# Projections of x and of the mixer's output in fp32r parts, on one Trainium2 core

## What is computed

```python
h = rms_norm(x, norm_mix_g)
proj = h @ w_in                     # 1024 x 2304: q, k, v (512 each), x_rg, gate_rg, q_ca (256 each)
o_sb = stick_breaking_attention(...)   # 8 heads of 64, strictly causal
o_rg = gelu(gate_rg) * rg_lru(conv(x_rg))
o_ca = memory_cross_attention(q_ca, mem, ...)  # 4 heads, softmax over 256 memory tokens
y = concat([rms_norm(o_sb, g_out_sb), rms_norm(o_rg, g_out_rg), rms_norm(o_ca, g_out_ca)])
x = x + y @ w_out                   # 1024 x 1024
x = x + moe_ffn(rms_norm(x, norm_ffn_g), ...)  # 64 experts (3 MB each), top 8 a token, one shared
```

## Time and profile before

| | us |
|---|---|
| runs | 619.40, 619.62, 621.31; median 619.62 |
| profiled execution | 622.31, its span on the core 620.5 |
| TensorE busy | 568.3 (92%), weight loads 368.6 |
| VectorE, ScalarE, GpSimd busy | 202.0, 139.7, 20.3 |
| transfers | 228.1 MB, mean 368 GB/s |
| chain that ended last | TensorE 57%, transfers 24%, SP's queue 12% |

### The profile page before, as it was taken

The page is one execution under the profiler, slowest core; times in us unless marked ns, Lnnn a source line. Parts: engine busy times, 40 slices in busy tenths (PEclk is TensorE's granted clock), DMA queues, the critical chain, the costliest instruction groups (busy, mean ns, idle before and its releaser), DMA issues.

```text
span 620.5 us, 9982 instructions
## 1 busy us (share of the span) xinstructions
PE 568.3 (92%) x4044; PEld 368.6 (59%) x4045; DVE 202.0 (33%) x516; ACT 139.7 (23%) x263; POOL 20.3 (3%) x78
## 2 busy tenths in 40 slices
PE   7999998999999998995999999899988999599775
PEld 5888774457566556662676565656655665356351
DVE  2247686777225222221222212112222122022102
ACT  4454246343111111110111101111111111011101
POOL 1003131000000000000000000000000000000000
PEclk8999999999999999997899999999999999899987
DMA  8995359633899999999999999999999999999992
GB/s 341 424 393 205 136 222 360 285 120 145 345 397 388 383 423 421 420 421 422 421 421 419 420 421 417 421 423 420 421 420 421 420 421 421 421 420 419 421 372 94
DMA packets 34143, 228.13 MB, mean 368 GB/s; under 512 B 3888, under 2 KB 4016, under 8 KB 8624
## 3 DMA queue, kind: packets, MB, share of 16 engines
q1 hardware_dynamic: 33952, 227.46, 89.5%
q10 hardware_dynamic: 144, 0.02, 0.0%
HBM read 226.42 MB, written 1.05 MB: 367 GB/s over the span
## 4 chain that ended last, share of the span: by engine, by line
PE 57%; DMA 24%; SPq 12%; ACT 2%; DVE 2%; issue 2%; ACTq 0%
DMA cell_gu<-in_w_up_e 16%; PE ps L1584 16%; SPq L355 9%; PE ps L1606 9%; PE ps L1336 7%; PE ps L1558 5%; DMA cell_gu<-in_w_gate_e 5%; PE ps L1614 5%; PE ps L1458 4%; PE ps L1353 4%; DMA cell_d<-in_w_down_e 2%; PE ps L1505 2%; PE ps L1343 1%; SPq L452 1%; DMA wA<-in_w_qk 1%
## 5 line engine op out<-in xcount | busy, mean ns | idle before, releaser
L1584 PE MATMUL ps<-cell_gu,xg 128*64 128x256 f32 (+2 forms) x2048 | 196.6, 404 | 30.2 <-DMA cell_gu<-in_w_up_e 20.0
L1584 PEld LDWEIGHTS ps<-cell_gu,xg 128*64 128x64 f32 (+2 forms) x2048 | 127.5, 133 | 106.0 <-issue 59.0
L1606 PE MATMUL ps<-cell_d,e_hT 128*64 128x512 f32 (+2 forms) x512 | 96.6, 611 | 5.0 <-issue 3.6
L1221 DVE TENSOR_TENSOR e_h<-e_sg,ps 128x256 f32<-128x256 f32 x26 | 16.1, 619 | 197.2 <-ACT e_sg L754 197.2
L1282 DVE SCALAR_TENSOR_TENSOR ylo<-ps,gslot,yhi 128x512 fp32r<-128x512 f32 x52 | 39.0, 751 | 121.7 <-ACT yhi L768 121.7
L1606 PEld LDWEIGHTS ps<-cell_d,e_hT 128*64 128x64 f32 (+2 forms) x512 | 28.2, 127 | 59.1 <-issue 56.4
L768 ACT ACTIVATE yhi<-ps,gslot 128x512 fp32r<-128x512 f32 x52 | 35.7, 687 | 121.8 <-PE ps L1606 121.8
L754 ACT ACTIVATE e_sg<-ps 128x256 f32<-128x256 f32 x26 | 10.0, 384 | 219.8 <-PE ps L1584 219.8
L1558 PE MATMUL ps<-pick,xhi 128*128 128x256 f32 x208 | 45.3, 299 | 1.1 <-DVE pick L1139 1.1
L1614 PE MATMUL ps<-yhi,S 128*128 128x512 f32 x104 | 43.3, 417 | 0.6 <-DVE ylo L1282 0.6
L1558 PE MATMUL ps<-pick,xlo 128*128 128x256 f32 x208 | 41.9, 283 | 0.0
(11 more groups left out here) (315 smaller groups left out, 496.6 us busy)
## 6 DMA issues: line engine op xcount, KB each, us to landing
cell_gu<-in_w_gate_e SPq DMA_DIRECT2D x64, 1024.0 KB, 26.2
cell_gu<-in_w_up_e SPq DMA_DIRECT2D x64, 1024.0 KB, 26.6
cell_d<-in_w_down_e SPq DMA_DIRECT2D x60, 1024.0 KB, 27.2
wA<-in_w_qk SPq DMA_DIRECT2D x8, 512.0 KB, 10.6
wo<-in_w_out SPq DMA_DIRECT2D x1, 4096.0 KB, 13.3
cell_d<-in_w_down_e SPq DMA_DIRECT2D x8, 512.0 KB, 17.3
wR<-in_w_rest SPq DMA_DIRECT2D x3, 1024.0 KB, 28.0
wV<-in_w_v SPq DMA_DIRECT2D x1, 2048.0 KB, 17.6
```

What stands on the lines that cost most here:

```text
L1221: nc.vector.tensor_tensor(dst[:].rearrange("q k p -> q p k"), e_sg[:].rearrange("q (p k) -> q p k", k=KH), ps[:, U, DE:2 * DE].rearrange(" ...
L1584: last = mm(ps[side * w:(side + 1) * w, U, cols], rows(k, slice(side * w, (side + 1) * w)), cell_gu[i][:, k, :], start=k == 0, stop=k == K ...
L1606: last = mm(ps[side * w:(side + 1) * w, Y[half], :], e_hT[:, kk, side * w:(side + 1) * w], cell_d[n][:, kk, half * 512:(half + 1) * 512], ...
```

## The change

Twelve blocks of x (2 to 7, 10, 11, 14 to 17) no longer run as fp32 products. Their weights are split: ScalarE casts the high part (`split_q`, `split_r`), GpSimd subtracts it and leaves the low part in the weight's own place. The two parts of `hT` lie side by side in one tile `h_both`, so that one fp32r product of 512 columns makes high by high and high by low at once, in the two halves of the bank, and one of 256 columns adds low by high to the first half. VectorE sums the two halves (`reduce_sum`) before it scales. Block 10's bank is now emptied by VectorE instead of ScalarE.

The output projection runs in three fp32r terms. ScalarE's scaling of y writes the high part, VectorE makes the low part (`low_y`), `split_o` casts the weights' high part into cells 8 to 11 of the ring, four casts of 1024 elements a partition in the walk behind `gelu` and one behind each softmax head, and GpSimd subtracts. In GpSimd's program the adds of squares of the first group move ahead of the last four subtractions, and the building of the order tables behind them.

Loads move: expert 1's gate and up go to other cells, and wait for block 1 and the squares of x; down of experts 1 and 2, and expert 3's gate and up, go behind block 17; expert 4's gate and up, and down of experts 3 and 4, behind the output projection.

```diff
-    cell_of = dict(zip(loads, [0, 1, 16, 4, 17, 5, 3, 2, 6, 9, 7, 10, 8, 11, 12, 13, 14, 15]))
+    cell_of = dict(zip(loads, [0, 1, 6, 4, 7, 5, 3, 2, 16, 9, 17, 10, 8, 11, 12, 13, 14, 15]))
...
+    h_both = at("h_both", o_ring + 16 * KB, [P, 2, KD, SEQ], F32R)
+    hT_hi, hT_lo = h_both[:, 0], h_both[:, 1]
...
+    wo_hi = [at(f"wo_hi{k}", o_ring + (72 * KB + 4 * KB * k if k < 6 else 40 * KB + 4 * KB * k), [P, D], F32R) for k in range(KD)]
...
-        walk = [("unit", 0), ("unit", 1), ("row", 0), ("unit", 2), ("unit", 3), ("unit", 4), ("split_w", 0), ("unit", 5),
-                ("split_w", 1), ("unit", 6), ("mem_norm", 0), ("unit", 7), ("split_a", 1)]
+        walk = [("unit", 0), ("unit", 1), ("split_q", 2), ("row", 0), ("split_q", 3), ("unit", 2), ("split_q", 4), ("unit", 3),
+                ("split_q", 5), ("split_q", 6), ("unit", 4), ("split_w", 0), ("split_q", 7), ("unit", 5), ("split_w", 1), ("unit", 6),
+                ("mem_norm", 0), ("unit", 7), ("split_r", 2), ("split_a", 1)]
...
-            walk += {2: [("split_w", 2)], 3: [("split_w", 3)], 5: [("log1p", 0)], 7: [("ca_square", 0)], 8: [("ca_norm", 0)], 9: [("conv", 0)],
-                     11: [("gelu", 0)]}.get(i, [])
+            walk += {2: [("split_w", 2)], 3: [("split_w", 3)], 5: [("split_r", 0), ("log1p", 0)], 6: [("split_r", 1)], 7: [("ca_square", 0)], 8: [("ca_norm", 0)], 9: [("conv", 0)],
+                     11: [("gelu", 0), ("split_o", 0), ("split_o", 1)], 12: [("split_o", 2), ("split_o", 3)]}.get(i, [])
...
+            sp.wait_ge(unit_ps, 2)
+            sp.wait_ge(alo_dve, 1)
             load_fixed("gate", 1)
+            sp.wait_ge(ssq_act, 2)
             load_fixed("up", 1)
...
             sp.wait_ge(wo_ps, len(projections))
+            load_fixed("gate", 4)
+            load_fixed("up", 4)
+            load_fixed("down", 3)
+            load_fixed("down", 4)
             load_fixed("gate", 5)
...
+            def split_q(n):
+                pool.wait_ge(part_hi_act, n - 1)
+                pool.tensor_tensor(wA_lo[n][:], wA[n][:], wA_hi[n % 4][:].bitcast(F32), ALU.subtract).then_inc(part_lo_pool, 1)
+
+            def split_r(g):
+                pool.wait_ge(part_hi_act, (8, 9, 7)[g])
+                for c in (slice(0, 4), slice(4, 8)):
+                    hi, lo = (w2_both[:, 0, c, :], w2_both[:, 1, c, :]) if g == 2 else (wR_hi[g][:, c, :], wR_lo[g][:, c, :])
+                    pool.tensor_tensor(lo, wR[g][:, c, :], hi.bitcast(F32), ALU.subtract).then_inc(part_lo_pool, 1)
+
+            def split_o(k):
+                pool.wait_ge(part_hi_act, 10 + k)
+                pool.tensor_tensor(wo_lo[:, k, :], wo[:, k, :], wo_hi[k][:].bitcast(F32), ALU.subtract).then_inc(part_lo_pool, 1)
...
+            pool.wait_ge(ysq_act, 4)
+            link(pool.tensor_tensor(y_sq[:, 0:2, :], y_sq[:, 0:2, :], y_sq[:, 2:4, :], ALU.add))
+            pool.tensor_tensor(y_sq[:, 0, :], y_sq[:, 0, :], y_sq[:, 1, :], ALU.add).then_inc(ysum_pool, 1)
+            for k in range(4, KD):
+                split_o(k)
...
+                    if n in IN_PARTS:
+                        src = dst
+                        link(nc.vector.reduce_sum(src, b.rearrange("p (i s) -> p s i", i=2), AX.X))
+                    nc.vector.tensor_tensor(dst, src, rstd_row[:], ALU.mult).then_inc(unit_dve, 1)
...
+                    for k in range(KD):
+                        mm(b, hi[:, k, c:c + P], h_both[:, :, k, :], start=k == 0, stop=k == KD - 1, skip_group_check=True)
+                        last = mm(b[:, 0:SEQ], lo[:, k, c:c + P], hT_hi[:, k, :], start=False, stop=k == KD - 1,
+                                  skip_group_check=True)
...
-                        pe.wait_ge(yg_act, k + 1)
-                    last = mm(ps[:, ACC[2 * t + half], :], yT[:, k, t * P:(t + 1) * P],
-                              wo[:, k, half * 512:(half + 1) * 512], start=k == chunks[0], stop=k == chunks[-1])
+                        pe.wait_ge(alo_dve, 1 + KD + k + 1)
+                        pe.wait_ge(part_lo_pool, 12 + k + 1)
+                    q, c = slice(t * P, (t + 1) * P), slice(half * 512, (half + 1) * 512)
+                    for m, (y, w) in enumerate(((yT_hi[k][:, q], wo_hi[k][:, c]), (yT_lo[:, k, q], wo_hi[k][:, c]),
+                                                (yT_hi[k][:, q], wo_lo[:, k, c]))):
+                        last = mm(ps[:, ACC[2 * t + half], :], y, w, start=k == chunks[0] and m == 0,
+                                  stop=k == chunks[-1] and m == 2)
```

More of the change, by code:

```diff
@@ L178, in hybrid_decoder_layer @@
     yT = r("yT", [P, KD, SEQ])
+    yT_lo = at("yT_lo", r.offset - KD * SEQ * 4, [P, KD, SEQ], F32R)
+    yT_hi = [at(f"yT_hi{k}", (o_V + 12 * KB if k < 4 else o_R + 12 * KB) + KB * (k % 4), [P, SEQ], F32R) for k in range(KD)]
     x1 = at("x1", o_O, [P, NT, D])
@@ L413, in _ @@
             sp.dma_start(x1[:], x[0].rearrange("(t p) d -> p t d", p=P)).then_inc(x1_loaded, 16)
+            sp.wait_ge(unit_ps, 18)
+            load_fixed("down", 1)
+            load_fixed("down", 2)
+            load_fixed("gate", 3)
+            load_fixed("up", 3)
             sp.wait_ge(o_ps, SB_HEADS)
@@ L418, in _ @@
             load_shared("up")
[L419 to L424, removed]
             sp.wait_ge(unit_ps, 26)
@@ L507, in _, with edges @@
             pool.memset(grp[:], HUGE).then_inc(consts, 1)
[L509 to L516, removed]
-            for kind, h in walk:
+            def edges():
+                pool.wait_ge(xT_act, KD // 2)
+                pool.wait_ge(xT_dve, KD // 2)
+                pool.wait_ge(alo_dve, 1 + KD)
+                for b in range(2):
+                    link(pool.memset(rest[b][:, P:P + 1], 1.0))
+                    last = pool.memset(rest[b][:, NZ + 1:NZ + 2], 1.0)
+                    link(last)
+                pool.memset(stat[:, 15:16], 0.0).then_inc(zeroed, 1)
+            def split_q(n):
[9 more added lines that the diff above has]
+                pool.tensor_tensor(wo_lo[:, k, :], wo[:, k, :], wo_hi[k][:].bitcast(F32), ALU.subtract).then_inc(part_lo_pool, 1)
+            for kind, h in walk:
+                if kind == "split_o":
+                    split_o(h)
+                if kind == "split_q":
+                    split_q(h)
+                elif kind == "split_r":
+                    split_r(h)
                 if kind != "z":
                     continue
+                if h == 0:
+                    edges()
                 pool.wait_ge(bc_act, 2 * h + 2)
@@ L637, in split_w, with split_q, split_r @@
                 nc.scalar.copy((wV_hi, w_kv_hi)[i // 2][:, c, :], (wV, w_kv)[i // 2][:, c, :]).then_inc(whi_act, 1)
+            def split_q(n):
+                act.wait_ge(wA_loaded[n], 16)
+                if n >= 6:
+                    act.wait_ge(unit_ps, n - 3)
+                nc.scalar.copy(wA_hi[n % 4][:], wA[n][:]).then_inc(part_hi_act, 1)
+            def split_r(g):
+                act.wait_ge(wR_loaded[g], 16)
+                act.wait_ge(unit_ps, 8 if g == 2 else 12)
+                nc.scalar.copy(w2_both[:, 0] if g == 2 else wR_hi[g][:], wR[g][:]).then_inc(part_hi_act, 1)
             split_a(0)
@@ L1339, in unit @@
                     if n in (10, 11):
-                        pe.wait_ge(wR_loaded[2], 16)
+                        pe.wait_ge(part_lo_pool, 8)
                         c = (n - 10) * P
                         for k in range(KD):
-                            last = mm(b[:, 0:CA], hT[:, k, c:c + P], wR[2][:, k, :], start=k == 0, stop=k == KD - 1)
+                            mm(b, hT_hi[:, k, c:c + P], w2_both[:, :, k, :], start=k == 0, stop=k == KD - 1, skip_group_check=True)
+                            last = mm(b[:, 0:CA], hT_lo[:, k, c:c + P], w2_both[:, 0, k, :], start=False, stop=k == KD - 1,
+                                      skip_group_check=True)
                     else:
```

91 lines of the change are left out of this document (58 added, 33 removed).

## The result

The changed kernel takes 654.5 us (median; the kernel before on the same chips 620.4): ratio 1.055, interval 1.053 to 1.058. The forecast was 627.6 with a range of 619.5 to 634.0. The sign was right, the size was not: 34 us were lost where 8 were expected.

A forecast was written before the change was run, and what follows sets the result against it. The mixer's end, when group 0's gate product frees cells for the weights' stream, sets the time. Block 33 +9 and pairs -1.3 gave 7.8, taken as 8.0: 619.6 + 8.0 = 627.6 us, range 619.5 to 634.0.

The forecast's parts named there:

- the fixed rest: After group 0's gate product frees its cells: remaining weights' stream and tail, so each mixer microsecond is one of the result.
- ScalarE's start on y: Before the output projection: two VectorE sums, 1.4 us, delay y's block 2, so ScalarE begins at 90.6, +0.8 us.
- TensorE's saving: Blocks of x save 8.1 us and the output projection 6.4, together 14.5 us, if nothing else is late.
- rival (c): Whole mixer: low parts always ready, TensorE stays the bound; 14.5 us less, 605.1; chance 0.13, whole or in part.
- (a): Mixer: GpSimd and VectorE don't disturb each other; block 33 at about 119.8, total 621.1, 1.5 us slower; chance 0.18.
- To the first scores: 0: Start to first scores, 42.97 before: block savings offset by waits for low parts; 0 taken, best -0.9, upper case +6.
- deciding point: Whether VectorE's product after block 2's sum starts on time: 0.4 us or up to 2.8, deciding between forecast and (b).
- GpSimd's pace: A GpSimd subtraction of 1024 elements takes 2.37 us, from 2.14 ns an element and 0.18 fixed.
- its chain: GpSimd from 93.9: subtractions, adds, subtractions, order tables, second group's add; 26.2 us to 120.1, ahead of block 33.
- TensorE's waits for low parts: TensorE idle ahead of output projection and block 33, GpSimd named as releaser; no such waits would prove the prediction wrong.
- The term of contention, 6 us: Last GpSimd chain: GpSimd stands still while VectorE reads two SBUF tiles; 6 us taken between 0 and 10.4.
- rival (b): GpSimd's subtractions also stop VectorE, 2.4 us at a time; first scores 6 us later, total 633.6; chance 0.20.

The follow-up runs named there:

- Fills: Changed kernel with GpSimd's 20 subtractions replaced by about equally long fills of zero that read nothing from SBUF, low parts left out: 633.3 us, ratio 1.020.

## Why the prediction was right or wrong

**What bounds the kernel, and the fixed rest: right.** The end of the mixer moved by 34.3, the time by 34; the window behind it is 23.7 us in both, and the moved loads are hidden. Wrong is where the 8 us of the mixer were to come from. The forecast had ScalarE's start on y 0.8 us later, measured are 12.4 (102.2 for 89.77); it had the end of GpSimd's add for the second group about 10 us later, measured are 33.5 (149.2 for 115.69).

**TensorE's saving: right in size for a pair, wrong in where it would count.** A pair of products takes 0.352 us after (starts at 28.16, 28.51, 28.86) for 0.348 forecast. The output projection's saving was put too high: its four groups of three products take 2.84 us in the kernel without subtractions (100.90 in its chain), for 2.7 forecast and 3.44 before, so it is 0.15 a group rather than 0.2. How far the saving can get shows in the kernel without subtractions. ScalarE starts on y at 83.85 there, for 89.77 before, so 5.9 us had been won. Then come these (ScalarE's timeline, and the chain of waits):

```profile
86.33 3.87 ACT L707 CAST wo_hi<-wo 128x1024 fp32r<-128x1024 f32 x4
```

```profile
93.84 2.23 DVE yT_lo L1096 x3
```

The four casts stand ahead of the gates' sigmoids. These start at 91.51, for 93.31 before: of the 5.9 us, 4.1 are gone. The low parts of y stand ahead of the projections, and these ahead of the softmax scores in TensorE's queue: the first row maximum is at 98.15, for 97.87 before, and the rest is gone too. The first exponential (99.08, before 99.30) and the second group's add of squares (115.13, before 114.97) are level. So rival (c), 605.1, was out of reach for any speed of GpSimd in this order of work: free low parts of the weights give 622.3. I had both in the sum, but as something behind which GpSimd was later still. That the two alone eat the gain I hadn't drawn; the nearest case, (a), gave 621.1 for another reason.

**"To the first scores: 0": the first step that failed.** They start at 48.37 instead of 42.97. The text had this very case as its upper bound, +6, by "two or three times 2.4 us" in front of the memory parts, and measured are +5.4, with `wV_lo` (+2.2) and `memT_lo` (+3.8) in the chain. I took the lower end since the trace of before showed VectorE slowed by 0.09 us at most. (The deciding point that I had named, VectorE's product after block 2's sum, takes 1.93 us, at 21.22 in its timeline, for 0.42.) The row that gave the 0.09 had GpSimd instructions of 0.29 us beside it. It spoke of what short instructions do. An instruction that is stopped is stopped until the other one ends, and the change made that length eight times larger.

**GpSimd's pace: right, 5% too low; its chain: wrong.** 2.37 us were forecast for 1024 elements, by a line through two sizes; measured are 2.489, the mean of six, and 2.499, of eight. That the chain behind y would set the end was wrong: in the changed kernel the second group's add of squares comes at

```profile
148.49 0.73 POOL L601 TENSOR_TENSOR y_sq<-y_sq 128x256 f32<-128x256 f32 x1 [0.72 <-ACT y_sq L701]
```

released by ScalarE's square, not by the tables or subtractions ahead of it, which had ended 0.72 us before. GpSimd also had idle time in the chain that I drew without a gap: its four last subtractions wait 7.5 and 4.8 us for casts, which stand behind exponentials that wait for VectorE's `mx`. And TensorE's waits for low parts, whose absence was to be a sign of being wrong, come to 3.6 us.

**The term of contention, 6 us: the step of the sum that failed by most.** It was worked out as what GpSimd loses to VectorE's instructions, bounded by 10.4. What VectorE loses to GpSimd's was left out of it, although it is the larger side: 31 us more busy time, and 32.5 us of time (622.3 to 654.8) where TensorE waits for none of the subtractions. And rival (b) had it in kind, with the right sign and the right deciding point (a product beside a subtraction takes 2.5 us instead of 0.43: row `beta` above), but counted it only up to the first scores, +6. It works in every stage of the mixer in which a subtraction runs: the convolution +5.9 (three of its six `xc` take 2.4 to 2.5 us, for 0.484), the little chain of `lam` +6 (L903, L911 and L912 at 2.0, 2.3 and 2.3 for 0.16 to 0.17), the row maxima and `ca_p`. 20 subtractions of 2.5 us are 50 us in which such an instruction can't run, and the question to ask was how many of VectorE's instructions would come up in them. The windows of before had much of the answer. VectorE was busy for 29.0 of the 40 us from 60 to 100 and for 12.8 of 16 from 101 to 117, so beside most of the last 12 subtractions one would be waiting; between 14 and 31, where the six of blocks 2 to 7 run, it was busy for 5.2 of 17.

**What came on top.** Behind TensorE's pauses its granted clock was lower. It has no product between 40.5 and 48.4 us; the clock is 1.00 until 44, 0.50 (the level of 1.2 GHz) from 46 to 50 and 1.00 again from 52. Over longer stretches of the changed kernel it is 0.83 between 40 and 60 us and 0.79 between 100 and 133 (the value ahead of the last two); without the subtractions it is 1.00 and 0.95 there:

```profile
40.00:60.00 20.00, 12.13 (x59) 9.14 (x57) 12.30 (x18) 9.13 (x16) 7.99 (x15) 0.83 0.41 156
...
100.00:133.00 33.00, 17.70 (x88) 11.73 (x86) 29.09 (x37) 17.79 (x34) 16.65 (x8) 0.79 0.54 216
```

The block of 24 products that starts at 50.03 took 6.52 us, for 5.67 in the kernel without subtractions. No experiment separated what the lower clock costs; it lies inside the 32 us.

Open is how much of the time goes to each kind of hold in the changed kernel. Of its 31 us of longer VectorE instructions 8.9 are in those with one input; that is busy time, and no run shows what they cost by themselves. Fills cost 11 us for their lateness and their hold together.

## What to carry to other kernels

Work that is put on GpSimd because it is idle isn't free if VectorE is busy beside it: count the whole lengths of its instructions that read SBUF as time in which VectorE's instructions with two SBUF inputs stand still (here `tensor_scalar` from SBUF to SBUF did too), and also ask whether that engine's queue stands in front of what TensorE waits for. A rival for which the trace has only short instructions as evidence must be priced by the length that the change brings, over every stage it brings it to. And to learn what a helper's work costs, run it with the bounding engine not waiting for it, and then leave it out: two such runs tell lateness from contention.

## What was unexpected of the hardware

- An instruction on 128x2 elements took 2.32 us instead of 0.16 beside a GpSimd subtraction of 128x1024; one on 128x256 elements took 2.45 instead of 0.48. Both lost about 2 us, whatever their own work.
- GpSimd's fills, which read nothing, left VectorE's two-input instructions at 0.484 us, and yet held a one-input one (SBUF to SBUF) for up to 1.63 us instead of 0.17.
- Cutting the long instruction in four cut each stop to about 0.65 us, but gave back only 5 of the 34 us.
